# Another pace in the plan of a convolution's products, and the place of a few transfers

## Time and profile before

| | us |
|---|---|
| median of three timed runs | 1814.56 (1813.0 to 1815.45) |
| the profiled execution | 1814.31 |
| its span, first to last instruction | 1812.5 |
| PE busy | 1734.8 (96%) |
| DVE busy | 1187.3 (66%) |
| ACT busy | 834.6 (46%) |
| POOL busy | 588.7 (32%) |
| mean granted clock of TensorE | 0.992 of full speed |

### The profile page before, as it was taken

How to read it: one execution, slowest core, us unless ns; L and a number is a source line. 1 busy time by engine, 2 the same in 40 slices (tenths; PEclk the granted TensorE clock), 3 DMA queues, 4 the chain that set the end, 5 groups by cost and what they waited for, 6 DMA issues and landing times.

```text
span 1812.5 us, 24678 instructions
## 1 busy us (share of the span) xinstructions
PE 1734.8 (96%) x9105; PEld 1413.2 (78%) x9105; DVE 1187.3 (66%) x1820; ACT 834.6 (46%) x1645; POOL 588.7 (32%) x434
## 2 busy tenths in 40 slices
PE   7999998999999889999999999899999999999998
PEld 6898888888899668788888887667777777777776
DVE  6478887897998558688787332565545665655652
ACT  6655556555335553323232322454444544444442
POOL 2499999999548012222323111100000000000000
PEclk9999999999999989999999999999999999999999
DMA  6311111021221754543535243652223222223211
GB/s 208 107 54 41 47 56 55 29 72 39 71 74 60 253 176 147 170 156 119 166 108 173 101 141 107 204 166 72 68 78 98 73 97 74 74 85 94 85 50 41
DMA packets 157405, 185.25 MB, mean 102 GB/s; under 512 B 55109, under 2 KB 120749, under 8 KB 153148
## 3 DMA queue, kind: packets, MB, share of 16 engines
q1 hardware_dynamic: 152972, 171.96, 29.7%
q10 hardware_dynamic: 4320, 11.80, 1.6%
HBM read 115.82 MB, written 70.72 MB: 103 GB/s over the span
## 4 chain that ended last, share of the span: by engine, by line
PE 56%; POOL 24%; DVE 8%; DMA 4%; ACT 4%; issue 3%; SPq 1%; POOLq 0%; DVEq 0%; ACTq 0%
POOL a_csum L477 21%; PE c_acc L121 19%; PE b_pso L121 11%; PE b_psq L121 8%; PE c_pss L2038 4%; PE c_psp L2047 3%; PE c_pso L2062 3%; DVE a_pst L628 2%; POOL a_csum L474 2%; PE a_ps L734 1%; POOL b_hrs L1003 1%; PE b_pst L1324 1%; DVE b_x L1183 1%; DMA q_d<-b_qo 1%; PE c_pso L2056 1%
## 5 line engine op out<-in xcount | busy, mean ns | idle before, releaser
L734 PE MATMUL a_ps<-a_xt,a_wring 128*128 128x512 f32 (+3 forms) x2880 | 562.1, 356 | 19.7 <-ACT a_zo L539 7.0
L734 PEld LDWEIGHTS a_ps<-a_xt,a_wring 128*128 128x128 f32 x2880 | 498.1, 191 | 77.3 <-ACT a_zo L539 8.7
L477 POOL TENSOR_TENSOR a_csum<-a_prod,a_csum 128x704 f32<-128x704 f32 (+1 forms) x231 | 404.7, 1752 | 39.9 <-ACT a_prod L526 6.4
L628 DVE SCALAR_TENSOR_TENSOR a_pst<-a_vbuf,taps,a_pst 128x704 f32<-128x704 f32 (+1 forms) x338 | 314.1, 929 | 10.4
L526 ACT ACTIVATE a_prod<-a_vbuf,taps 128x704 f32<-128x704 f32 (+1 forms) x252 | 215.0, 863 | 170.6 <-POOL a_csum L477 158.1
L121 PE MATMUL b_pso<-w,b_yt 128*128 128x512 f32 (+1 forms) x816 | 192.3, 395 | 1.2 <-DVE b_yt L1177 1.2
L121 PE MATMUL c_acc<-w,c_ht 128*128 128x512 f32 x768 | 186.2, 398 | 0.1
L121 PEld LDWEIGHTS b_pso<-w,b_yt 128*128 128x128 f32 (+1 forms) x816 | 151.4, 187 | 35.5 <-DVE b_yt L1177 1.4
L121 PEld LDWEIGHTS c_acc<-w,c_ht 128*128 128x128 f32 x768 | 143.5, 190 | 36.5 <-issue 7.1
L1655 ACT ACTIVATE c_pt<-c_psp 128x1024 f32<-128x1024 f32 (+1 forms) x64 | 63.9, 998 | 140.5 <-PE c_psp L2047 140.5
L1649 ACT ACTIVATE c_s<-c_s,c_nm 128x256 f32<-128x256 f32 (+1 forms) x256 | 124.5, 488 | 0.0
(11 more groups left out here) (197 smaller groups left out, 2343.4 us busy)
## 6 DMA issues: line engine op xcount, KB each, us to landing
ht_d<-b_ht SPq DMA_DIRECT2D x16, 1024.0 KB, 4.1
c_ht<-ht_d SPq DMA_DIRECT2D x16, 1024.0 KB, 4.9
a_stage<-in_w_in_a SPq DMA_DIRECT2D x24, 512.0 KB, 4.1
a_x<-in_x_prompt SPq DMA_DIRECT2D x16, 512.0 KB, 3.6
b_cz<-c_d SPq DMA_DIRECT2D x16, 512.0 KB, 4.9
b_cz<-z_d SPq DMA_DIRECT2D x16, 512.0 KB, 6.3
b_x<-in_x_prompt SPq DMA_DIRECT2D x16, 512.0 KB, 3.5
x_d<-b_x SPq DMA_DIRECT2D x16, 512.0 KB, 2.6
```

The lines of the kernel that those rows point to most:

```text
L477: pool.tensor_tensor(out, prod[:, (PTAPS * n + i) % RING, 0:t1 - t0], out, ALU.add).then_inc(prod_added, 1)
L628: dve.scalar_tensor_tensor(part if k == DTAPS - 1 and not last else here, vbuf[:, b % 2, t0 + k:t1 + k], wcol(k, b), part if k == 0 else h ...
L734: last = pe.matmul(out, wring[:, u % 3, a, k], xt[c][:, e, k, 0:n], start=(k == 0 and a == 0 and e == 0), stop=(k == KT - 1 and a == 1))
```

## The change

There are two edits. In `plan_conv` an addition is reckoned to take 2.25 ns a column and 260 ns instead of 2.2 and 170, and a product is put ahead of group i's sigmoid or copy only if it could start 3.0 us before the group's end, not 0.9. In stage B's SP stream the code for the old pieces moves from the head of a tile's body to the tail of the one before.

```diff
@@ plan_conv
         for i in range(1, PTAPS):
             add.append(now)
-            now += (2.2 * size(n) + 170) / 1e3
+            now += (2.25 * size(n) + 260) / 1e3
@@
-    p.products_by = [sum(t < end[i] - 0.9 for t in product) for i in range(p.count)]
+    p.products_by = [sum(t < end[i] - 3.0 for t in product) for i in range(p.count)]
@@ phase_b, sync
+        def load_old(e):
+            after(sp, old_step, TAPS * e)
+            sp.dma_start(vw, g.v_left[e * P:(e + 1) * P, :]).then_inc(old_in, 16)
+
@@ body(t, left, old)
-            if old is not None and old[1] == 0:
-                if old[0] == 0:
-                    sp.wait_ge(w.w_lo, 5 * KT)
-                else:
-                    store_old(old[0] - 1)
-                after(sp, old_step, TAPS * old[0])
-                sp.dma_start(vw, g.v_left[old[0] * P:(old[0] + 1) * P, :]).then_inc(old_in, 16)
-            if left is not None and left[0] == 0:
-                store_old(LEFT - 1)
-                sp.wait_ge(old_out, 16 * LEFT)
-                load_left(0)
-                load_left(1)
             if t == 4:
...
             if isinstance(t, int) and t == TILES:
                 return
+            if old is not None and old[1] == 1:
+                store_old(old[0])
+                if old[0] + 1 < LEFT:
+                    load_old(old[0] + 1)
+                else:
+                    sp.wait_ge(old_out, 16 * LEFT)
+                    load_left(0)
+                    load_left(1)
+            if t == 1:
+                sp.wait_ge(w.w_lo, 5 * KT)
+                load_old(0)
             if left is not None:
```

## The result

| | before | after |
|---|---|---|
| median of five runs each | 1814.56 (1809.51 to 1815.45) | 1799.99 (1798.05 to 1802.08) |
| ratio, 95% interval | | 0.9922 (0.9907 to 0.9937) |
| the profiled execution, its span | 1814.31, 1812.5 | 1798.05, 1796.2 |
| VectorE's last step of stage A starts (L626) | 586.69 | 573.41 |
| PE turns stage B's first tile | 595.16 | 581.86 |

What follows compares the result with a forecast made beforehand. POOL's additions were taken to pace stage A. POOL's 14.5 us advance at piece 17 plus 1.0 for one step, part 2 at 0, less 0.5 for PE's lateness, took 1814.3 to 1799.3; forecast 1796 to 1803, 8-in-10 range 1793 to 1809.

Steps and rivals of the forecast that it cites:

- Step 1: Stage A, ScalarE: fewer products before copies and sigmoids; copies 6 to 9 us earlier relative to PE, gaps to 313 go.
- Step 2: Stage A, POOL: VectorE runs up to POOL near group 60; 8 or 9 us late places, PE keeps 14 of 22.5.
- The place worked out in full: Step 234, opening piece 13, and the V5 gates after it: chunk 3 gate at 411.5, PE 3 us late.
- Step 3: Early sigmoid barrier at group 12: product 15 ends at 98.5, and POOL starves and loses 2.1 us.
- Rival A: POOL starves more, or VectorE reaches piece 15 later: 4 to 10 us more, time 1803 to 1810; chance 0.22.
- Step 4: Stage A's tail: POOL's 16.66 us idle goes, piece 17 starts at 462.9, and 15.5 us reach phase B.
- The collisions on SBUF: POOL additions beside VectorE splits or first steps: 36 over 1.9 us, 0.6 each, 22 in all; no change.
- The forecast's other case: Stage A collisions at their hardest: 16 splits each cost POOL 1.22, 10 us in all, leaving a gain of about 5.
- Part 2: SP's transfers, code moved between tile ends: the stream written out is the same, cost 0.
- B: Slower: barriers starve POOL, 0.9 us each; decides from 20 of 51 on, 25 give 1820, 35 give 1829; chance 0.06.
- C: Nothing changes: transition weights' transfers or the V7 gate are bound by PE and VectorE; 1811 to 1817; chance 0.07.
- D: The whole ceiling of PE's stage A loss is gained, as additions collide less: 22.5 us, 1792; chance 0.05.

Runs made afterwards that it cites:

- experiment 1: The kernel before with only the change's SP transfer code, planner as before: 1814.22, ratio 1.0008.
- experiment 2: The kernel before with only the new pace of an addition (2.25 ns a column, 260 ns), old 0.9 us margin: 1800.03, ratio 0.9922.
- 11: The changed kernel with PTAPS 12 for 13 (fewer POOL additions, more VectorE steps) and lists filled from group 113 on: 1800.04, ratio 0.9929.
- 12: The changed kernel with additions reckoned at 370 ns for 260, 0.9 us margin up to group 14, lists filled from group 113: 1799.30, ratio 0.9923.
- experiment 8: The changed kernel with POOL's additions from a piece's second on cut to 512 columns, the rest of the sum left out: 1784.50, ratio 0.9845.
- experiment 7: The kernel before with POOL's additions from a piece's second on cut to 512 columns, the rest of the sum left out: 1787.78, ratio 0.9862.
- experiment 10: The changed kernel with the 0.9 us margin up to group 14 and all five V7 gates 3 to 7 VectorE steps earlier: 1793.63, ratio 0.9892.

## Why the prediction was right

- **Step 1, ScalarE comes free.** Right in direction: VectorE's split wait is 14.7 (said: under 20). But ScalarE is less late, not free, as the new plan too is faster than POOL (the forecast's 22.1 and 20.4 a piece against 22.8). Three sizes were off. The z copies of groups 50 to 54 were to come 6 to 9 us sooner behind their groups; the first two did (16.2 to some 9.2), the other three by 0.4 to 0.8 (11.5 to 11.0 on average). ScalarE's wait on POOL was to fall under 150 and is 167.2: as POOL takes a product each 1.8 us in either plan, ScalarE waits for it as often, only with the other work done first. And PE's gaps up to 313 were to go: two remained, 0.68 and 0.86 at 296.08 and 301.37, both behind copies of Z2.
- **Step 2, POOL is what is late next.** Right: VectorE's waits on POOL rose from 13.3 to 29.5 us. They begin at piece 4 (189.46), not near group 60, so VectorE runs up to POOL sooner than reckoned. V4's and V5's gates are 12 us behind PE, as said. The place worked out in full was right in its times (gates at 401.43 and 411.81, for 401 and 411.5) and wrong in its price: PE waited 0.40 us there, not 3, since it was itself later than reckoned. The gaps from 340 us on came to 5.1, for 8 to 9.
- **Step 3, starving.** The mis-sized term. I had 2.1 us at one place; it was 3.2 there (0.69 and 2.47). Product 15 ended at 99.2 and not at 98.5, since behind the barrier ScalarE first did the next weight split (97.41, 1.05 us), which I had left out. Of the loss 1.9 was left when piece 2 ended (144.12 for 142.22). And 1.6 more came before piece 18 (1.19 and 0.45), which I did not have. The 1.19 is no barrier: the piece's first product waited for V6's chunk 3 gate, which VectorE made late, behind its own waits on POOL:

```profile
483.84 0.98 ACT L526 ACTIVATE a_prod<-a_vbuf,cols,taps 128x704 f32<-128x704 f32 x1 [3.64 <-DVE a_vbuf L648]
```
Rival A was this at 4 to 10 us; the starving came to 4.8 in all, 2.7 over my term, and the links of step 4 are late by some 2.
- **Step 4, the tail.** Each link is within 2.2 us of its forecast (given in brackets), and the excess is step 3's: additions of piece 16 end 463.6 (462.9); piece 17 starts 463.55 without idle (462.9); V6's chunk 1 gate 460.16 (458.3); piece 18 ends 509.37 (507.4); V7's chunk 1 gate 527.41 (525.4); last step 573.41 (571.2); PE at the middle of group 116 578.1 (578.8). So PE waited 3.75 us for the tile and not the 0.9 forecast, and the tile came at 581.86, for 579.7. The sum was 15.0; the stage gave 13.3, and the profiled execution 16.3 with 3 us of scatter behind it. That the medians gave 14.6, within half a us of the sum, is luck: the terms were off by 2.
- **The collisions on SBUF.** The forecast let them stay as many, and they did: 36 of the 252 additions took over 1.9 us in either profile, and all 252 took 441.4 us in both. The price was read wrong. In before the 19 of them with a split beside them lost 0.85 us each and the 17 with a piece's first step 0.47, 24 us in all; the forecast had 0.6 for each and 22. A pair in after:

```profile
416.39 2.35 DVE L609 TENSOR_TENSOR a_wring<-a_stage,a_wring 128x1024 fp32r<-128x1024 f32 x1 [1.06 <-ACT a_wring L514]
```
```profile
417.62 2.54 POOL L474 TENSOR_TENSOR a_csum<-a_prod 128x640 f32<-128x640 f32 x1
```
The split takes 1.22 and such an addition 1.57 where each is alone. The Trainium skill, "SBUF — State Buffer", Who interferes with whom, calls what the two engines share an exclusive lock; these rows agree with that to some tenths of a us. The forecast's other case, a gain of about 5, did not follow from it: whatever a collision costs, before pays it as well as after.
- **Part 2.** Nothing, as read from the code: experiment 1 has it at 1.0008, and from stage B's first load on SP issues the same 382 transfers in the same order in before, experiment 1 and after.
- **The rivals.** B (slower) would have needed 20 starving barriers; POOL starved behind three (93.49, 99.31, 487.82). C (nothing changes) fell with the result, and experiment 2 shows which edit it was. D's ceiling of 1792 was passed neither here nor by experiments 11 and 12, which removed all of PE's gaps from 70 us on: its 22.5 us were PE's, and PE's gaps are not what the end hangs on.

What stays open: how much of the 14 us of experiment 8 is the tail and how much collisions with VectorE, and what 11 and 12 would have given without the filled lists.

## What to carry to other kernels

An order written out by hand or by a planner puts a slow engine's pace into the queues of all others: reckon with the measured pitch from start to start, hand-over included, since a plan that is 0.12 us too fast at each of 252 additions let whole groups wait behind products that could not yet run. Count a gain at the transition where the stage's last result leaves, not by the idle time of the busiest engine; here removing 6 us of PE's gaps gave nothing, and five gates moved on an engine that was never the fullest gave some 4 (7 with the early margin put back). Where one instruction is moved forward, move the ones that its consumers wait for next as well, or the gain turns into a new wait some us later.

## What the runs showed of the hardware

- Cutting GpSimd's additions to 512 columns (experiment 7) took all gaps from PE, and 25 us from the old kernel, though the earlier trace rows had POOL idle for 38 us in the tail: an engine at 32% of the span was the one that set stage A.
- PE's gaps of 3.76 and 2.10 us in before were each followed by a stretch at the lower granted level: the mean granted clock was 0.71 over the 9.75 us from 159.03 and 0.77 over the 7.34 us from 358.55, and 2.4 and 1.6 us were lost. The gap of 2.26 ahead of 284.73 was followed by none (clock 1.00, 5.71 us for 24 matmuls of 512 columns), so the length of the one gap does not decide it. After has no gap over 1.47 us between 150 us and the tile, and no such stretch. Behind the tile's gap of 3.75 the clock was 0.51: the first eight matmuls took 1.92 us, where they took 1.03 without a gap in experiment 10, and the 36 that follow 9.30 for 8.43. So after's wait for the tile costs 1.8 us more than its length.
